# Triangular inverses of a chunked DeltaNet kept packed to the end, with 32x32 and 64x64 products for the last two levels

## The reference

```
decay = exp(where(incl, gc[c] - gc[s], -inf))
a_mat = where(strict, beta[c] * (k k^T) * decay, 0) + I
sol   = triangular_solve(a_mat, [beta * v, beta * exp(gc) * k])       # u0, w
step: u = u0 - w S;  o = qg S + qk u;  S = S * exp(gc_last) + kg^T u
```

## Time and profile before

| | us |
|---|---|
| median of 3 runs | 1557.67 (1556.09 to 1560.55) |
| profiled execution, its own time | 1557.05 |
| its span | 1555.2 |
| PE busy | 1477.3 (95%) |
| DVE busy | 1043.3 (67%) |
| ACT busy | 601.4 (39%) |
| POOL busy | 154.1 (10%) |

### The profile page before, as it was taken

One profiled execution on the slowest core, in us unless ns is written; L12 is line 12 of the kernel. 1 busy time (PEld: TensorE's weight loads), 2 busy tenths in 40 slices (PEclk: granted clock), 3 DMA queues, 4 the chain that ended last, 5 costly groups with the idle time before them and its releaser, 6 DMA issues.

```text
span 1555.2 us, 29812 instructions
## 1 busy us (share of the span) xinstructions
PE 1477.3 (95%) x11798; PEld 1373.2 (88%) x11798; DVE 1043.3 (67%) x1943; ACT 601.4 (39%) x1180; POOL 154.1 (10%) x148
## 2 busy tenths in 40 slices
PE   6899999999999999999997878899999999999998
PEld 2799999999999999987785667899999999998886
DVE  4977777787365757553877887678887777753333
ACT  4522222221123533443556434354544444444223
POOL 0000000000000000020003545764000000000000
PEclk9999999999999999999996878999999999999999
DMA  9345444545244312211102100012123222221222
GB/s 341 102 144 151 142 152 149 154 143 161 82 149 136 96 46 77 59 55 42 42 2 62 43 30 16 22 53 71 55 59 91 81 81 86 81 77 69 81 68 95
DMA packets 174582, 141.85 MB, mean 91 GB/s; under 512 B 8464, under 2 KB 156437, under 8 KB 173461
## 3 DMA queue, kind: packets, MB, share of 16 engines
q1 hardware_dynamic: 151652, 117.89, 24.4%
q10 hardware_dynamic: 22833, 22.59, 4.6%
HBM read 137.01 MB, written 3.45 MB: 90 GB/s over the span
## 4 chain that ended last, share of the span: by engine, by line
PE 83%; DVE 10%; issue 3%; ACT 2%; SPq 1%; DMA 1%; POOL 0%; DVEq 0%; ACTq 0%
PE ps L2326 15%; PE ps L2328 14%; PE ps L2327 14%; PE ps L2478 5%; PE ps L2476 5%; PE ps L2477 5%; PE ps L2548 3%; PE ps L2547 3%; PE ps L2546 3%; PE ps L2756 1%; PE ps L2879 1%; PE ps L2909 1%; PE ps L2777 1%; PE ps L2923 1%; PE ps L3001 1%
## 5 line engine op out<-in xcount | busy, mean ns | idle before, releaser
L2326 PE MATMUL ps<-h_hi,w_lo 128*128 128x320 f32 x1152 | 364.7, 317 | 11.7 <-DVE h_lo L1429 4.5
L2328 PE MATMUL ps<-h_hi,w_hi 128*128 128x320 f32 x1152 | 356.9, 310 | 0.0
L2327 PE MATMUL ps<-h_lo,w_hi 128*128 128x320 f32 x1152 | 356.9, 310 | 0.0
L1382 DVE TENSOR_TENSOR w_lo<-w_raw,w_hi 128x1024 fp32r<-128x1024 f32 x120 | 147.7, 1233 | 228.9 <-ACT w_hi L748 228.6
L2326 PEld LDWEIGHTS ps<-h_hi,w_lo 128*128 128x128 f32 x1152 | 217.4, 189 | 18.5 <-DVE h_lo L1429 7.2
L2327 PEld LDWEIGHTS ps<-h_lo,w_hi 128*128 128x128 f32 x1152 | 217.6, 189 | 0.8 <-issue 0.2
L2328 PEld LDWEIGHTS ps<-h_hi,w_hi 128*128 128x128 f32 x1152 | 217.2, 189 | 0.0
L748 ACT CAST w_hi<-w_raw 128x1024 fp32r<-128x1024 f32 x120 | 125.6, 1048 | 197.3 <-PE ps L2328 107.8
L1516 DVE SCALAR_TENSOR_TENSOR ada_acc<-ada_ffn,cond,ada_acc 128x256 f32<-128x256 f32 x392 | 161.7, 478 | 1.2
L2326 PE MATMUL ps<-act_hi,w_lo 128*128 128x320 f32 (+1 forms) x352 | 108.9, 309 | 2.1 <-DVE mods L1545 2.1
L2328 PE MATMUL ps<-act_hi,w_hi 128*128 128x320 f32 (+1 forms) x352 | 108.5, 308 | 0.0
(11 more groups left out here) (413 smaller groups left out, 3015.8 us busy)
## 6 DMA issues: line engine op xcount, KB each, us to landing
w_raw<-in_w_ffn_in SPq DMA_DIRECT2D x64, 512.0 KB, 3.8
w_raw<-in_w_ffn_out SPq DMA_DIRECT2D x44, 512.0 KB, 3.8
ada_ffn<-in_w_ada ACTq DMA_DIRECT2D x43, 512.0 KB, 4.0
w_raw<-in_w_in SPq DMA_DIRECT2D x28, 512.0 KB, 3.7
ada_ffn<-in_w_ffn_in SPq DMA_DIRECT2D x20, 512.0 KB, 3.7
ada_k<-in_w_ada SPq DMA_DIRECT2D x8, 1024.0 KB, 11.1
ada_ffn<-in_w_ada SPq DMA_DIRECT2D x13, 512.0 KB, 3.4
w_raw<-in_w_out SPq DMA_DIRECT2D x8, 512.0 KB, 3.3
```

What stands on the lines that cost most here:

```text
L1382: nc.vector.tensor_tensor(w_lo[at], w_raw[s][:], w_hi[at].bitcast(F32), ALU.subtract)\
L2326: nc.tensor.matmul(out, lo, xh, start=start, stop=False)
L2327: nc.tensor.matmul(out, hi, xl, start=False, stop=False)
L2328: return nc.tensor.matmul(out, hi, xh, start=False, stop=stop)
```

## The change

- Levels 0 to 4 stay packed, but the unturned and the turned copy now stand side by side in t_cols (index 1 and 0), and one DVE operation of 256 columns masks both into tt_cols. POOL's masks go, and so do the arrays t_c and the five 128x128 masks; the last set of constants holds sides5 packed and a half6 mask of 64 columns.
- Level 5 is done on the packed 32x32 blocks: outer_first (16 products with blocks of m_t beside the diagonal), ACT negates (x_w index 2), outer_second and outer_turned (16 products each, giving the new block and its turned copy), and outer_own (4 products with a 32x32 identity) puts the old blocks beside them in PSUM. A PSUM bank then holds T and its turned copy as 64x64 blocks; one DVE mask (half6) takes both to tt_cols.
- Level 6 is two calls of eight 64x64 products (last_first, last_second) with a negation by ACT between. ACT and DVE copy the blocks to t_all with 64-row copies. The turn on PE and all 128x128 products of the inverses are gone.
- k k^T and k q^T come in one call at stage k = 2, neighbouring products on different row halves and in different banks, and DVE reads them across two banks.
- A unit has 20 stages; starts are 0, 4, 8, 13, 20, 24, 28, 33, 40, 44. Its counts are PE_T, DVE_T, ACT_T, POOL_T = 15, 25, 8, 1. 204 products a unit (before 156, more of them large).
- ACT's part of the first scan step, Silu and table loads move into its list of stages. Whoever waited for DVE's end of a unit waits for ACT's too. w_low moves from THREE_DONE + 9 to + 8.

The core of the diff:

```diff
-PE_T, DVE_T, ACT_T, POOL_T = 17, 28, 5, 8
+PE_T, DVE_T, ACT_T, POOL_T = 15, 25, 8, 1
-MAKE_STAGES = 21
-MAKE_START = [0, 4, 8, 13, 21, 25, 29, 34, 42, 46]
+MAKE_STAGES = 20
+MAKE_START = [0, 4, 8, 13, 20, 24, 28, 33, 40, 44]
...
                     if r >= 1:
-                        sp.wait_ge(t_pe[c], r * PE_T - d)
+                        sp.wait_ge(t_pe[c], r * PE_T - 4 * d)
...
# ACT
+                    if c == THREE_DONE + 1:
+                        act.wait_ge(kv_copied, 2 * NT + 2)
+                        for b in range(4):
+                            scan_kg(0, b)
+                    if c in (THREE_DONE + 2, THREE_DONE + 3):
+                        for i in range(2 * (c - THREE_DONE - 2), 2 * (c - THREE_DONE - 1)):
+                            nc.scalar.activation(z_t[:, i, :], z_t[:, i, :], ACT.Silu)
+                    if c == THREE_DONE + 3:
+                        load_power_table()
+                    if c == THREE_DONE + 8:
+                        w_high(TILE_WOUT, 0)
+                    if THREE_DONE + 4 <= c < THREE_DONE + 8:
+                        scan_first(c - THREE_DONE - 4)
...
+                if k == 16:
+                    act.wait_ge(t_pe[c], r * PE_T + 10)
+                    nc.scalar.activation(x_w[c][:, 2, :], ps[:, 2 * c, 0:P], ACT.Copy, scale=-1.0).then_inc(t_act[c], 1)
+                if k == 18:
+                    act.wait_ge(t_pe[c], r * PE_T + 14)
+                    nc.scalar.activation(x_w[c][:, 2:4, :].rearrange("p a n -> p (a n)"), ps[:, 2 * c, 0:256],
+                                         ACT.Copy, scale=-1.0).then_inc(t_act[c], 1)
+                    act.wait_ge(t_dve[c], r * DVE_T + 24)
+                    for a in range(0, P, DK):
+                        ins = nc.scalar.copy(heads4(t_all[a:a + DK, t, g, :], P)[:, :, a:a + DK],
+                                             heads4(ps[a:a + DK, 2 * c + 1, 256:512], DK))
+                    ins.then_inc(t_act[c], 1)
...
# DVE
-                    nc.vector.tensor_tensor(t_c[:, c, :], t_c[:, c, :], ps[:, bank, 0:P], ALU.subtract).then_inc(t_dve[c], 1)
+                    nc.vector.tensor_tensor(t_now, t_now, ps[:, bank + 1, 0:P], ALU.subtract).then_inc(t_dve[c], 1)
...
-                    nc.vector.transpose(x_turned, t_c[:, c, :]).then_inc(t_dve[c], 1)
+                    nc.vector.transpose(t_cols[c][:, 0, :], t_now).then_inc(t_dve[c], 1)
                     dve.wait_ge(t_dve[c], dve0 + 6 + 4 * n)
-                    if n < 4:
-                        nc.vector.tensor_tensor(subs(t_cols[c][:, 0, :]), subs(x_turned), packed(f"sides{n + 1}"),
-                                                ALU.mult).then_inc(t_dve[c], 1)
-                    else:
-                        nc.vector.tensor_tensor(in_blocks(t_cols[c][:]), each_block(x_turned), block_mask("sides5"),
-                                                ALU.mult).then_inc(t_dve[c], 1)
...
+                    nc.vector.tensor_tensor(subs(t_sides), subs(t_pair), packed(f"sides{n + 1}", 8), ALU.mult).then_inc(t_dve[c], 1)
+                if k == 17:
+                    dve.wait_ge(t_pe[c], pe0 + 13)
+                    half6 = const("half6")[:, None, 0:DK].broadcast_to([P, 8, DK])
+                    nc.vector.tensor_tensor(tt_cols[c][:].rearrange("p a n -> p (a n)").rearrange("p (h n) -> p h n", n=DK),
+                                            heads4(ps[:, bank + 1, :], DK), half6, ALU.mult).then_inc(t_dve[c], 1)
+                if k == 19:
                     dve.wait_ge(t_pe[c], pe0 + 15)
+                    for a in range(0, P, DK):
+                        ins = nc.vector.tensor_copy(heads4(t_all[a:a + DK, t, g, :], P)[:, :, DK - a:2 * DK - a],
+                                                    heads4(ps[a:a + DK, bank, 256:512], DK))
+                    ins.then_inc(t_dve[c], 1)
...
# PE
+            def products(t, g, c):
+
+                for at, which in ((0, 4), (256, 0)):
+                    for h in range(4):
+                        out = ps[:, 2 * c + h % 2, at + (h // 2) * P:at + (h // 2 + 1) * P]
+                        ins = nc.tensor.matmul(out, qk(t, g, h, 4), qk(t, g, h, which), start=True, stop=True)
                 ins.then_inc(t_pe[c], 1)
...
+            def outer_first(c):
+                for h in range(4):
+                    for a in range(0, P, SUB):
+                        o = a ^ SUB
+                        ins = nc.tensor.matmul(blocks_of(ps[:, 2 * c, 0:P], o, h), m_t[c][a:a + SUB, h, o:o + SUB],
+                                               blocks_of(tt_cols[c][:, 0, :], a, h), start=True, stop=True)
+                ins.then_inc(t_pe[c], 1)
...
+            def outer_own(c):
+                for a in range(0, P, SUB):
+                    half = a // SUB % 2 * SUB
+                    out = heads4(ps[a:a + SUB, 2 * c + 1, :], DK)[:, :, half:half + SUB]
+                    ins = nc.tensor.matmul(out, unit_ident(a), subs(t_cols[c][a:a + SUB, 0:2, :]), start=True, stop=True)
+                ins.then_inc(t_pe[c], 1)
...
+            def last_first(c):
+                for h in range(4):
+                    for a in (0, DK):
+                        o = DK - a
+                        ins = nc.tensor.matmul(ps[o:o + DK, 2 * c, h * DK:(h + 1) * DK], m_t[c][a:a + DK, h, o:o + DK],
+                                               sides6(c, 0, a, h), start=True, stop=True)
+                ins.then_inc(t_pe[c], 1)
...
+                if k == 16:
+                    pe.wait_ge(t_dve[c], dve0 + 23)
+                    outer_first(c)
+                    outer_own(c)
+                if k == 17:
+                    pe.wait_ge(t_act[c], act0 + 6)
+                    pe.wait_ge(t_pe[c], pe0 + 11)
+                    outer_second(c)
+                    pe.wait_ge(t_pe[c], pe0 + 12)
+                    outer_turned(c)
                 if k == 18:
+                    pe.wait_ge(t_dve[c], dve0 + 24)
+                    last_first(c)
+                if k == 19:
+                    pe.wait_ge(t_act[c], act0 + 7)
+                    last_second(c)
```

219 lines of the change are left out of this document (98 added, 121 removed).

## The result

The kernel after takes 1546.55 us (median of 4 runs, 1545.23 to 1551.22) where before took 1559.11 on the same chip: 12.6 us less, ratio 0.9926 [0.9897, 0.9955]. A second series of six runs, beside the experiment e17, gave 1548.10, ratio 0.9942 [0.9927, 0.9957]. Forecast were 1523 us and a range of 1508 to 1546. The sign was right; nearly two thirds of the expected gain is missing. The profiled execution took 1551.22 us with a span of 1549.3.

What follows compares the result with a forecast made beforehand. The prediction took PE and DVE, waiting on each other in turns at reduced clock, as the bound. Fill -11, middle round -14, last stretch -11, together -36, plus 2 for decays: 1557.05 becomes 1523 us, range 1508 to 1546.

Steps and rivals of the forecast that it cites:

- DVE: VectorE's work per unit: 12.6 us before, 9.5 to 10 after; a round of four units 39 us, before 50.8.
- PE: TensorE's work per unit at full clock: 11.0 us before, 8.5 after; at half clock 18.3 before, 12.8 after.
- Rival (c): 64x64 products and outer_own do not run side by side on TensorE; slower, 1587 us, at full clock 1531; 4%.
- ACT, POOL, DMA: Other engines and transfers: ACT 7.2 us a unit, far below DVE's 10; POOL's new waits nothing; decays fit by little.
- The 2 us for the decays: Decay loads in the units' loop: 5.8 us needed, 6.3 there, so 2 us added over the kernel.
- rival (b): In-order waits for decays and ACT hold a loop stage at 2.5 us instead of 2.3; -17 us, 1540; 15%.
- Stages: Middle round: a pair of stages 4.2 to 4.4 us; round 43 at full clock, 52 at half, 47 taken.
- the fill: Stretch from 832.06 to 876.76: 44.7 us before, 34 after, TensorE work 31.4 at half clock; -11.
- The last stretch: Stretch from 937.82 to 1000.0: 62.2 us before, 51 after, 42 busy and 9 idle; -11, at half clock +8.
- (a): Clock stays at 1.2 GHz through the whole loop; fill -11 + 2, round -8, last stretch +8: 1548 us; 12%.
- What would show it: Signs: round 47 us, DVE busy 38 to 40, 256-column masks 0.42, no DVE wait for PE above 2, scan 66.
- The bounds set for "wrong": Middle round above 55 us, PE clock 0.5 there, or DVE idling for ACT or decays over 1 us a unit.

Runs made afterwards that it cites:

- e17: e10 with ScalarE's split of the first output weights at THREE_DONE + 4 instead of + 7; 1541.7 us, ratio 0.9868.
- e8: Before, with the joined 256-column masks of the inner levels alone, GpSimd's packed masks of these levels gone; 1568.5 us, ratio 1.0055.
- e2: After, with each inner call made of four 32x32 products over 128 moving columns instead of sixteen over 32 (inverses not computed); 1536.7 us, ratio 0.9867.
- e3: After, with each inner call made of one 128x128 product with the identity (inverses not computed); 1543.2 us, ratio 0.9911.
- e4: After, with the decays of units 4 to 9 loaded to one partition instead of 128; 1545.6 us, ratio 0.9924.
- e7: After, with the first output weights split earlier: ScalarE's half at THREE_DONE + 4, VectorE's at + 7, instead of + 8; 1544.9 us, ratio 0.9910.
- e9: After, with one unused dense 128x128 product behind each inner call from stage 36 on; 1543.0 us, ratio 0.9902.
- e10: After, with all units started 5 stages apart and the output weights' split at THREE_DONE + 7; 1536.8 us, ratio 0.9857.
- e16: e10 with e2's inner calls of four wide products instead of sixteen small ones (inverses not computed); 1524.0 us, ratio 0.9760.
- e6: After, with GpSimd's burst of four last masks spread over four stages; 1550.2 us, ratio 0.9931.
- e12: After, with e9's late dense products, e7's earlier weight split and products() cut in two halves; 1554.9 us, ratio 0.9962.
- e14: Before, with units started 5, 5, 5, 6 stages apart and w_low at THREE_DONE + 7; 1560.1 us, ratio 0.9997.
- e15: e10 with e9's dense extra products from stage 36 on; 1534.9 us, ratio 0.9823.
- e1: After, with one unused dense 128x128 product behind each of a unit's eight inner calls; 1554.6 us, ratio 0.9997.

## Why the prediction was wrong, by its steps

**DVE, right.** 10.1 a unit, 39 a round, 256-column masks 0.42: measured 39.2 in the round, and 0.42 and 0.45 for the two kinds of mask. The joined masks by themselves made before slower (e8).

**PE, sizes right.** last_first and last_second take 0.68 a call at full clock and 1.12 at half (forecast 0.75), outer_own's last four records 0.74 at half. Between two such calls the products, 1.16 and 2.08:

```profile
881.73 0.68 PE L2922 MATMUL ps<-spare 64*64 64x64 f32 x16 [0.52 <-DVE spare L2117]
882.73 1.16 PE L2862 MATMUL ps<-pre 64*128 64x128 f32 x16
...
893.12 2.08 PE L2862 MATMUL ps<-pre 64*128 64x128 f32 x16
895.13 1.12 PE L2922 MATMUL ps<-spare 64*64 64x64 f32 x16
```

Rival (c) falls: the 64x64 pairs share a PSUM bank and eight take 0.68, where eight 128x64 take 2.00. The shorter weights could be part of that. The plainer case is e2: four products from four different groups of 32 rows, 128 moving columns each, go to one bank, each to its own 32 partitions, in 0.42 us at full clock, where e3's single product of 128 moving columns takes 0.49. The rule of the Trainium skill, "TensorEngine Tiling (Array Packing)", Gotcha 1, that different row tiles cannot use one PSUM bank at the same time, is not borne out by this trace.

**ACT, POOL, DMA, right in the middle.** ACT 28.0 / 4 = 7.0 (forecast 7.2). The 2 us for the decays were not needed (e4); rival (b) falls. That w_high and w_low move was left uncosted; TensorE stops 3.05 us at the first product with these weights, but e7 and e17 show that shortening this stop brings nothing measurable.

**Stages, the step that failed.** It priced a pair of stages by durations alone, 4.2 to 4.4 us, hence "full clock: 43 a round", 47 with clock. It named the clash (three of four units have their heavy stage at once) and charged little for it, and took TensorE's cost as busy time, so that 1628 records a round were as good as 1233. Measured: 52.9 and 54.1, with TensorE idle for 14.0 us of the first. The missing 6 to 7 us are more than covered by instruction supply and uneven order, each mostly hidden while the other stands; without both the round is 44.8. How much the clock, which I had made the main uncertainty of the round, moves it is not shown: at 0.77 (e3) and 0.70 (e2) it is 50.7 and 50.6, but e3's calls are longer.

The same step failed in the fill. Its sum took TensorE as the limit, 31.4 us of work at half clock and 34 in all (the terms do not quite fit their own words: with 2.5 for every unit's products and one more last call for unit 1 they give 32.9). Measured are 24.8 us of work at a clock of 0.64, and 13.3 us in which TensorE stands: 38.1.

**The last stretch, wrong sign, and the larger part of the miss.** The three stretches miss 25 us of the -36: 4 in the fill, 6 in the round, 15 here. -11 was taken, +8 worked out for half clock; +4.1 came, at 0.61. The failed term is the work at full clock: 42 us busy and 9 idle were taken, 52.7 and 13.6 measured. TensorE is busy for 15.00 of 15 us in 957.79 to 972.79, at half clock, so there a lower clock is paid in full; e9 at 0.86 had 59.4. That still is 8 us above the forecast 51. e10 and e16 suggest that order and instruction supply act here too (60.2 and 57.4 at a clock of 0.7). How much GpSimd's burst costs stays open: e6 moved it without removing it. Why the clock comes back in e9 and not in e12 stays open as well.

**Rivals.** (a) had the right numbers (-9, -8, +8, 1548; measured -6.6, -8.2, +4.1, 1546.6) and half of the reason: right for the last stretch, though the clock there was 0.61 and not 0.50; in the middle, at 0.66, its -8 came with stops and an uneven order that it did not have. That its 1548 fits so well is in part luck. It deserved more than 12%.

**What would show it.** Busy times, masks, calls and scan came out as listed. The bounds set for "wrong" (round above 55, clock 0.5) were not crossed, though the round lies above the 52 given for half clock; the other sign that spoke was the waits of DVE for PE above 2 us, forecast absent: the longest is 2.3 in the round and 3.7 outside it.

## What to carry to other kernels

Many small TensorE products have a price that their busy time does not show: count the instructions of a stretch and set them against the rate at which they arrive. In a list that several units march through in one order, give equal parts of a step different stages; a change of spacing (e10, 1536.8 us) brought nearly as much as the whole rewrite of the levels, but only after that rewrite (e14). Where two limits of a stretch stand close together, removing one shows less than it is worth (2.2 and 2.3 us of the round alone, 8.1 together); remove both before a theory is dropped. And look at how a kernel's own runs scatter before a difference between two profiles is explained.

## What the runs showed of the hardware that was not expected

- TensorE's instructions arrive in 16 KB blocks of 128 matmul records with their loads; a stretch that runs them faster stops in mid-call, 0.3 to 2.6 us each, and gets a block each 3.5 to 3.9 us where it stops at one block after another (after and e10; e2, with a quarter of the instructions in its inner calls, has none in them). The queue's packets count the same: 13 for 1628 records, 10 for 1233, 7 for 868.
- Four 32x32 products of 128 moving columns, from four groups of rows into one PSUM bank, take 0.42 us (e2), one 128x128 product of 128 moving columns 0.49 (e3).
- Joining two 128-column masks into one of 256 on VectorE made the kernel slower (1.0055 [1.004, 1.007]) while GpSimd's 512-column masks ran beside it: 0.63 us each instead of 0.42, where the single ones take 0.46 to 0.50 instead of 0.30. At 0.74 for 0.83 the clock was lower too.
- The granted clock of a full stretch could not be set by adding dense products: 0.86 in e9, 0.79 in e15 and 0.68 in e12 for the last stretch, 0.72 in e1 for the middle.
- The same kernel spreads by 19 us with its clock: 1526.5 us at 0.969 and 1545.9 at 0.957 (e17).
